# Moving the output projection's pieces into pairs in TensorE's order of a hybrid mixer kernel

## What is computed

```
h = rmsnorm(x, g_pre) * (1 + scale) + shift
proj = h @ w_in                      # q, k, v, gates of three mixers
attn = sliding_window_attention(...) * silu(ag)      # 512 channels
rwkv = rwkv7_mixer(...) * silu(rg)                   # 256 channels
gla  = gla_mixer(...) * silu(gg)                     # 256 channels
y = concatenate([attn, rwkv, gla]) @ w_out           # 1024 x 1024
x1 = x + gate * rmsnorm(y, g_post)
```

## Time and profile before

| what | us |
|---|---|
| median of 3 runs | 3717.32 |
| lowest and highest of them | 3714.79, 3723.7 |
| the profiled execution, its own time | 3715.48 |
| its span in the trace | 3713.6 |
| mean granted clock of TensorE, share of full speed | 0.987 |
| full periods of the mixers' stage (1 to 14) | 917 to 1540 in the span |

### The profile page before, as it was taken

The page is one execution under the profiler, slowest core; times in us unless marked ns, Lnnn a source line. Parts: engine busy times, 40 slices in busy tenths (PEclk is TensorE's granted clock), DMA queues, the critical chain, the costliest instruction groups (busy, mean ns, idle before and its releaser), DMA issues. The chain is left out here.

```text
span 3713.6 us, 68764 instructions
## 1 busy us (share of the span) xinstructions
PE 3559.7 (96%) x27852; PEld 2692.3 (72%) x27852; DVE 1959.5 (53%) x4802; ACT 1585.8 (43%) x3591; POOL 420.7 (11%) x689
## 2 busy tenths in 40 slices
PE   6999999978999999989999999999999999999998
PEld 5887777856666666568777887777886676676765
DVE  4223333337777777434678788666673343443332
ACT  2222332224444444213677666777753334443320
POOL 0000000004444444210000000000000000000000
PEclk9999999988999999999999999999999999999999
DMA  9111111133222222231111114121215212111121
GB/s 301 53 52 50 49 52 52 52 116 128 74 74 74 74 74 74 88 128 47 48 53 51 61 51 163 55 65 54 69 62 173 74 49 76 41 48 65 44 78 47
DMA packets 137250, 282.10 MB, mean 76 GB/s; under 512 B 26368, under 2 KB 85648, under 8 KB 130448
## 3 DMA queue, kind: packets, MB, share of 16 engines
q1 hardware_dynamic: 130208, 268.88, 20.5%
q0 software_dynamic: 2304, 8.39, 0.6%
q10 hardware_dynamic: 4464, 1.02, 0.1%
HBM read 181.78 MB, written 96.47 MB: 75 GB/s over the span
## 5 line engine op out<-in xcount | busy, mean ns | idle before, releaser
L2506 ACT ACTIVATE at_pT<-at_bank 128x512 f32<-128x512 f32 (+3 forms) x320 | 154.4, 531 | 574.2 <-PE at_bank L2401 573.8
L272 PEld LDWEIGHTS p_bank<-p_hT,w_in 128*128 128x128 f32 x3328 | 378.6, 193 | 12.1 <-issue 9.9
L272 PE MATMUL p_bank<-p_hT,w_in 128*128 128x128 f32 x3328 | 383.2, 276 | 2.1 <-ACT p_hT L365 2.1
L1907 PEld LDWEIGHTS p_bank<-p_hT,w_in_rest 128*128 128x128 f32 x3072 | 345.4, 192 | 14.0 <-issue 12.4
L1907 PE MATMUL p_bank<-p_hT,w_in_rest 128*128 128x128 f32 x3072 | 349.9, 276 | 1.3 <-DVE p_st L2184 1.3
L2029 ACT ACTIVATE p_r<-p_acc,p_mid 128x384 f32<-128x384 f32 (+13 forms) x224 | 292.8, 1307 | 59.4 <-DVE p_acc L2211 55.0
L278 PE MATMUL p_bank<-w_in,p_hT 128*128 128x512 f32 (+2 forms) x1024 | 312.3, 463 | 0.0
L2524 DVE CUSTOM_DVE_ANT_0 at_s<-at_bank,at_bias 128x512 f32<-128x512 f32 (+3 forms) x320 | 181.8, 606 | 189.5 <-PE at_bank L2388 182.9
L278 PEld LDWEIGHTS p_bank<-w_in,p_hT 128*128 128x128 f32 x1024 | 172.0, 191 | 117.2 <-issue 107.1
L1057 PE MATMUL b_banks<-b_wout,b_yT 128*128 128x512 f32 x512 | 248.0, 610 | 3.7 <-DVE b_yT L1390 2.2
L2442 PE MATMUL at_bank<-arena,at_y 128*128 128x512 f32 x512 | 245.4, 602 | 2.9 <-DVE at_y L2552 2.5
(11 more groups left out here) (400 smaller groups left out, 5848.3 us busy)
## 6 DMA issues: line engine op xcount, KB each, us to landing
stage<-p_st SPq DMA_DIRECT2D x16, 1856.0 KB, 5.9
arena<-stage SPq DMA_DIRECT2D x16, 1856.0 KB, 7.7
at_rest<-stage SPq DMA_DIRECT2D x16, 1280.0 KB, 6.0
stage<-p_pr SPq DMA_DIRECT2D x128, 128.0 KB, 1.8
p_ada<-in_ada_w SPq DMA_DIRECT2D x4, 2048.0 KB, 15.8
p_xt<-in_x SPq DMA_DIRECT2D x16, 512.0 KB, 3.4
b_x<-in_x SPq DMA_DIRECT2D x16, 512.0 KB, 3.4
x<-b_x SPq DMA_DIRECT2D x16, 512.0 KB, 2.9
```

The costliest lines, as they stand in the source:

```text
L272: last = mm(out, w_in[:, k, place(c):place(c) + P], hT[:, k, 1:P + 1], start=(k == 0), stop=(k == KD - 1))
L1907: last = mm(bank[:, m * P:(m + 1) * P], weights(k, c + m * P, c + (m + 1) * P), hTs[:, n % 2, k, :], start=(k == 0), stop=(k == KD - 1))
```

## The change

Pieces 0, 2, 4 and 6 of `dense` leave their places and stand directly ahead of pieces 1, 3, 5 and 7. Nothing else changes: the same instructions with the same operands and signals. The other engines' orders are unchanged. No DMA moves.

```diff
                         scores(a, 0)
-                    if valid(o):
-                        dense(o, 0)
                     if valid(a):
                         key_values(a)
...
                     if valid(o):
+                        dense(o, 0)
                         dense(o, 1)
                     if valid(a):
                         Z(a, 1)
                         gla_round(a, 0)
+                    if valid(a):
+                        XY_products(a, 1)
                     if valid(o):
                         dense(o, 2)
-                    if valid(a):
-                        XY_products(a, 1)
-                    if valid(o):
                         dense(o, 3)
...
                         XY_products(a, 4)
-                    if valid(o):
-                        dense(o, 4)
                     if valid(a):
                         Z(a, 5)
                         turn_ke(a)
                     if valid(o):
+                        dense(o, 4)
                         dense(o, 5)
                     if valid(a):
                         XY_products(a, 5)
                         gla_out(a)
-                    if valid(o):
-                        dense(o, 6)
                     if valid(a):
                         turn_attended(a)
                         update_and_weights(a)
                     if valid(o):
+                        dense(o, 6)
                         dense(o, 7)
```

More of the change, by code:

```diff
@@ L1087, in _ @@
                         gla_round(a, 0)
-                    if valid(o):
-                        dense(o, 2)
                     if valid(a):
@@ L1092, in _ @@
                     if valid(o):
+                        dense(o, 2)
                         dense(o, 3)
```

## The result

| | us |
|---|---|
| the changed kernel, median of 7 runs | 3728.16 |
| lowest and highest of them | 3726.88, 3732.33 |
| ratio to the kernel before, with its 95% interval | 1.0030 (1.0018 to 1.0042) |
| forecast and range | 3728.0 (3720 to 3736) |

The changed kernel is 10.8 us slower by the medians of 7 runs each (3728.16 - 3717.32), 0.30%. In the trace, the stage that was changed shows what the prediction said, step by step. Lines of the other engines' blocks are four lower in the changed kernel: 1349 is 1345, 1362 is 1358, 1366 is 1362, 1160 is 1156.

What follows compares the result with a forecast made beforehand. TensorE's own instruction stream sets the pace. Fourteen full periods at +0.87 us (+12.2) and period 15 at -0.8 give +11.4 us: 3726.9 from the profiled execution, 3728.7 from the median; forecast 3728, range 3720 to 3736.

Steps and rivals of the forecast that it cites:

- The price list: Period 0, same steps of tile a without `dense`: waits 0.31 us before line 909, 0.52 before line 923, 0.41 before 944.
- Its three terms: Growth of a full period where a wait appears: pieces 0 and 1 +0.19 us, 4 and 5 +0.40, 6 and 7 +0.47.
- the term of pieces 2 and 3: Gap from line 1027 to line 933: no wait appears, -0.19 us a period.
- 1.91 us for every lone piece: Cost on TensorE of a `dense` piece standing alone, against 1.72 us for each further piece in a row.
- The sum: Terms of a full period: -0.19 + 0.19 + 0.40 + 0.47 = +0.87 us, in 14 periods +12.2 us.
- the floors of the first rival: Terms without waits: -0.12 us for pieces 0 and 1, -0.25 for 4 and 5, +0.06 for 6 and 7.
- Its -0.8 us: Period 15: lines 962 and 963 go ahead of pieces 0 to 3, which end at 1547.5 instead of 1548.35.
- the line of 0.3%: What a measurement can tell from no change, 11 us; within it 0.48, slower by more 0.50, faster by more 0.02.
- the covers weren't needed: First rival: VectorE's results come in time at all three places, period -0.50 us, kernel 3709.5 us; waits mostly hidden, chance 0.07.
- the passage between tile shapes: A lone piece between 64- or 32-row tiles costs 0.19 us of 1.91 beyond its share of a longer run.
- The clock: Rival: idle times drop TensorE to half clock, up to 1.7 us a stretch, once a period 3752 us; chance 0.05.
- named as a sign: The sum is wrong if, among other signs, the clock's half-speed stretches change in number in any stage.

Runs made afterwards that it cites:

- the two fills: Changed kernel with state_addition(b, 0) ahead of key_values(a): period 45.10 us; changed kernel with join_Y ahead of gla_addition: period 45.02 us; both against 45.49.
- the fill failed: Changed kernel with turn_ke(a) ahead of Z(a, 5): period 46.20 us against 45.49, one execution 3739.59 us.
- the mirror: Kernel before with each pair placed where its first piece stood: period 46.44 us, one execution 3745.80 us.
- the run that filled its gap: Changed kernel with state_addition(b, 0) ahead of key_values(a), before line 909: period 45.10 us against 45.49.

## Why the prediction was right

*The bound.* TensorE's stream set the pace, and every change of the period was found on it, as a wait or as a passage between steps.

*The price list.* The main step was to read the waits of a period that has no `dense`, rather than to work them out. Its three terms came out to 0.01 us, and so did the term of pieces 2 and 3, which was read from a step without a wait. The runs with one pair each show that they add up, and the two fills show that two of them are waits which other work, or another order on VectorE, takes away. For the third (before Z of round 5) the fill failed for another reason, so that it was a wait is shown by its idle note and by its absence in the mirror, not by a filling of its own.

*What the terms are made of.* The prediction has 1.91 us for every lone piece. That holds between steps on smaller tiles. Piece 6 of the kernel before stands between two steps on 128*128 tiles (lines 1045 and 1014), and there it takes 1088.28 - 1086.57 = 1.71 us:

```profile
1086.57 1.88 PE L1057 MATMUL b_banks<-b_wout,b_yT 128*128 128x512 f32 x4
1088.28 0.60 PE L1014 MATMUL b_banks<-ident,arena 128*128 128x128 f32 x4
```

The sum is untouched, since it went by whole gaps. But it tells the growth apart: moving piece 6 saves no passage, so its +0.48 is all wait (0.47 went in the run in which VectorE sums Y first). Piece 0 saves the 0.20 of a passage and exposes 0.39 (what went in the run that filled its gap). For piece 4, +0.39 and a passage of 0.20 leave 0.59 us, by difference only. Each is 0.06 to 0.07 us more than its idle note. So the floors of the first rival were set too high at the two places that were filled: they were worked out as if the wait were as long as the note.

*Period 15.* Its -0.8 us came.

*The size.* 14 x 0.87 - 0.8 = 11.4 us was the sum; the medians differ by 10.8 us in the runs of one comparison, and by 10.0 against the larger set of 21 runs of the kernel before. Both lie inside the interval, 6.7 to 15.6 us. That the median came within 0.2 us of the forecast of 3728 is luck: the forecast was put between 3726.9 and 3728.7, and the runs of the changed kernel spread over 5 us. The forecast that the result would sit at the line of 0.3% held, and on which side of it it lies can't be told from these runs.

*The rivals.* That the covers weren't needed fell with the idle notes. Its part that holds is the passage between tile shapes: -0.20 us for pieces 2 and 3 alone, where no wait appears. The clock stayed at full in the mixers' full periods even at twice the idle time. What the prediction named as a sign but didn't price is the clock elsewhere. Stretches at 1.2 GHz behind the mixers made the changed kernel's one execution 5 us longer, so two profiles compared by span show 14.9 us, half as much again as the mixers account for. Had they fallen in the other execution, they would have hidden half of the effect.

## What to carry to other kernels

When independent work is spread through a dependent chain, each piece is cover for one wait. Grouping pieces saves a passage between tile shapes where the neighbours use smaller tiles (0.20 us here) and costs whatever wait lay under the piece (0.39 to 0.59 us here), so decide place by place. A period of a pipeline in which the spread work is absent, at its ends, is a price list for this, and it can be read before anything is built. Where a wait is shown, look first whether another step of the right length can fill it or whether the late engine merely does something else first; and before moving a step, check the buffer it writes as well as what it reads.

## What the runs showed of the hardware that was not expected

An idle note on a matmul row understated the wait wherever it could be checked. In the mirror run the step from line 866 to 955 became 0.33 us longer with a note of 0.20 (0.44 at its weight load), and two waits of 0.14 and 0.18 us in effect had no note on PE at all, only 0.24 and 0.32 on PEld. So a row of PE without a note can still hide a wait of this size, contrary to what is said of such rows ahead of the prediction. Distances from start to start and the PEld rows are to be read, not PE's notes alone.

The granted clock was 1.00 over the mixers' full periods with repeated idle times of 0.3 to 0.8 us, five in a period of 47 us, and with one of 1.07 us in the first. In stages that the change doesn't touch, the clock differed between two executions: 1.2 GHz in three places more and for longer in a fourth went with 2141.5 us instead of 2136.6.
